# Hyena and mLSTM mixer: shifted rows issued from ScalarE's queue, and a new order of VectorE and ScalarE work

## The reference

```python
def hyena_mixer(u, conv_w, w1, b1, w2, b2, w3, freq, d_skip):
    u = short_conv3(u, conv_w).astype(jnp.float32)      # rows t-1, t, t+1 times three weights
    v, x1, x2 = jnp.split(u, 3, axis=-1)
    h = hyena_filters(L, w1, b1, w2, b2, w3, freq)      # each order divided by its sum of magnitudes
    d = d_skip.astype(jnp.float32)
    z = x1 * (long_conv(v, h[0]) + d[0] * v)            # long_conv: FFT, product, inverse FFT
    z = x2 * (long_conv(z, h[1]) + d[1] * z)
    return z

def even_mixer(xm, w_in, ...):
    u = xm @ w_in                                       # 1024 x 3600: Hyena v, x1, x2; q, k, v, o; gates
    y_hy = hyena_mixer(u[..., :3 * HY_W], ...)
    ...
    h, C, n, m = mlstm_bidir(heads(q), heads(k), heads(v), gates, C0, n0, m0)
    h = rmsnorm(h.transpose(0, 2, 1, 3), ml_norm_g).reshape(B, L, ML_W) * jax.nn.sigmoid(o)
    y = jnp.concatenate([y_hy, h], axis=-1) @ w_out
```

## Time and profile before

| | us |
|---|---|
| median of three runs | 1374.52 (1371.89 to 1374.98) |
| the profiled execution | 1374.98, its span 1373.1 |
| PE busy | 1321.2 (96%) |
| DVE busy | 1045.9 (76%) |
| ACT busy | 816.6 (59%) |
| POOL busy | 75.6 (6%) |
| DMA | 408.14 MB, mean 297 GB/s |

### The profile page before, as it was taken

The page is one execution under the profiler, slowest core; times in us unless marked ns, Lnnn a source line. Parts: engine busy times, 40 slices in busy tenths (PEclk is TensorE's granted clock), DMA queues, the critical chain, the costliest instruction groups (busy, mean ns, idle before and its releaser), DMA issues.

```text
span 1373.1 us, 16270 instructions
## 1 busy us (share of the span) xinstructions
PE 1321.2 (96%) x6307; PEld 1032.8 (75%) x6307; DVE 1045.9 (76%) x1011; ACT 816.6 (59%) x920; POOL 75.6 (6%) x81
## 2 busy tenths in 40 slices
PE   5999988999999989999999999999999999999997
PEld 2676646788886777788888888888888888888875
DVE  0584787555446753788998898998988988988996
ACT  2444324533335374677767767776777777777663
POOL 1102100000002000000000000000000000000370
PEclk9999999999999989999999999999999999999998
DMA  9979997855556633599999999999999999999992
GB/s 349 347 254 313 325 335 254 284 187 184 184 184 198 216 130 125 182 318 365 365 352 351 346 347 366 366 347 338 345 356 362 365 357 331 348 363 366 342 351 92
DMA packets 289591, 408.14 MB, mean 297 GB/s; under 512 B 15342, under 2 KB 223497, under 8 KB 289445
## 3 DMA queue, kind: packets, MB, share of 16 engines
q1 hardware_dynamic: 282048, 391.23, 83.8%
q0 software_dynamic: 3904, 11.59, 2.8%
q10 hardware_dynamic: 3556, 4.21, 0.9%
HBM read 401.99 MB, written 1.87 MB: 294 GB/s over the span
## 4 chain that ended last, share of the span: by engine, by line
PE 84%; DVE 8%; DMA 4%; ACT 1%; issue 1%; SPq 0%; POOL 0%; DVEq 0%; ACTq 0%
PE bank L1908 81%; DVE w_lo L550 3%; DMA raw<-in_w_ada 2%; PE bank L2258 2%; DMA Gb<-arena 1%; DMA raw<-in_ev_w_in 1%; PE bank L1966 1%; ACT w_hi L543 0%; DMA Gb<-gate_rows 0%; SPq L657 0%; ACT arena L1169 0%; DVE sml L1723 0%; PE bank L2379 0%; PE bank L2416 0%; DVE arena L1649 0%
## 5 line engine op out<-in xcount | busy, mean ns | idle before, releaser
L550 DVE TENSOR_TENSOR w_lo<-raw,w_hi 128x2048 fp32r<-128x2048 f32 (+1 forms) x238 | 549.0, 2309 | 157.0 <-ACT w_hi L543 155.4
L543 ACT CAST w_hi<-raw 128x2048 fp32r<-128x2048 f32 (+1 forms) x238 | 451.5, 1898 | 121.7 <-PE bank L1908 82.7
L1908 PE MATMUL bank<-w_hi,x_hi 128*128 128x512 f32 x1072 | 431.1, 402 | 7.5 <-DVE x_lo L1336 2.3
L1908 PE MATMUL bank<-w_lo,x_hi 128*128 128x512 f32 x1072 | 420.4, 392 | 0.0
L1908 PE MATMUL bank<-w_hi,x_lo 128*128 128x512 f32 x1072 | 419.3, 391 | 0.0
L1908 PEld LDWEIGHTS bank<-w_hi,x_hi 128*128 128x128 f32 x1072 | 201.3, 188 | 53.2 <-issue 8.7
L1908 PEld LDWEIGHTS bank<-w_hi,x_lo 128*128 128x128 f32 x1072 | 201.5, 188 | 45.2
L1908 PEld LDWEIGHTS bank<-w_lo,x_hi 128*128 128x128 f32 x1072 | 201.7, 188 | 38.8 <-issue 0.2
L550 DVE TENSOR_TENSOR w_lo<-arena,w_hi 128x2048 fp32r<-128x2048 f32 x88 | 203.0, 2307 | 33.1 <-ACT w_hi L543 32.9
L543 ACT CAST w_hi<-arena 128x2048 fp32r<-128x2048 f32 x88 | 168.3, 1912 | 28.8 <-PE bank L1908 28.8
L1908 PE MATMUL bank<-w_hi,g_hi 128*128 128x512 f32 x440 | 175.0, 398 | 3.4 <-DVE g_lo L1607 3.4
(11 more groups left out here) (300 smaller groups left out, 963.5 us busy)
## 6 DMA issues: line engine op xcount, KB each, us to landing
raw<-in_moe_w SPq DMA_DIRECT2D x352, 512.0 KB, 5.5
arena<-in_moe_w SPq DMA_DIRECT2D x176, 512.0 KB, 5.6
raw<-in_w_ada SPq DMA_DIRECT2D x96, 512.0 KB, 6.6
raw<-in_ff_w SPq DMA_DIRECT2D x66, 512.0 KB, 4.5
raw<-in_ev_w_in SPq DMA_DIRECT2D x28, 512.0 KB, 7.7
raw<-in_at_w_qkv SPq DMA_DIRECT2D x12, 512.0 KB, 5.1
raw<-in_ev_w_out SPq DMA_DIRECT2D x8, 512.0 KB, 5.7
Gb<-gate_rows POOLq DMA_DIRECT2D x8, 512.0 KB, 5.0
```

Of the source, the lines that this page charges most:

```text
L543: nc.scalar.copy(w_hi[:, t % SPL, c], place[:, c]).then_inc(hi_ok, 1)
L550: nc.vector.tensor_tensor(w_lo[:, t % SPL, c], raw_slot(n)[0][:, c], w_hi[:, t % SPL, c].bitcast(F32), ALU.subtract).then_inc(lo_ok, 1)
L1908: return pe.matmul(out, lhsT, rhs, start=start, stop=stop)
```

## The change

Four things change. The four shift DMAs of each block go from GpSimd's queue to ScalarE's own (`shift_rows(w)`), right behind the copies of that block's projection out of PSUM. On ScalarE the copy of projection 2 moves ahead of the magnitudes, the high part of IN[4] behind the logarithm of the gates, and the square root of the head squares ahead of `new_n` and `stage_rows(1)`. On VectorE both `normalised` move behind the low part of IN[6], `short_conv(2)` and `(3)` ahead of `weighted(2)` and `(3)`, `short_conv(4)` and `(5)` to both sides of `hyena_gate(0)`, and the head squares behind `fft_product(3)`. On TensorE two groups of idle products go from 13 and 5 to 7 and 9.

```diff
@@ GpSimd
-                pool.wait_ge(tj_t, 7 + 2 * w + 2)
-                pool.wait_ge(sh_z, 2)
-                uw = u[:, :, HW * w:HW * w + HW]
-                for r0, r1 in ((0, 112), (112, P - 1)):
-                    gp.dma_start(earlier[r0 + 1:r1 + 1], uw[r0:r1]).then_inc(sh_l, 16)
-                    gp.dma_start(later[r0:r1], uw[r0 + 1:r1 + 1]).then_inc(sh_l, 16)
@@ ScalarE
+            def shift_rows(w):
+                if w == 0:
+                    eng.wait_ge(sh_z, 2)
+                else:
+                    eng.wait_ge(cv_ok, 2 * w)
+                eng.wait_ge(tj_t, 7 + 2 * w + 2)
+                uw = u[:, :, HW * w:HW * w + HW]
+                for r0, r1 in ((0, 112), (112, P - 1)):
+                    eng.dma_start(earlier[r0 + 1:r1 + 1], uw[r0:r1]).then_inc(sh_l, 16)
+                    eng.dma_start(later[r0:r1], uw[r0 + 1:r1 + 1]).then_inc(sh_l, 16)
...
+            take_proj(2, two_heads(qT, 1))
             eng.wait_ge(f_tap, 1)
             for r in range(2):
                 sc.activation(mags[:, r, :], taps[:, 2 * r, :], ACT.Abs)
                 sc.activation(magb[:, r, :], taps[:, 2 * r + 1, :], ACT.Abs).then_inc(f_abs, 1)
-            take_proj(2, two_heads(qT, 1))
-            high(IN[4])
             eng.wait_ge(g_in, 1)
             link(sc.activation(rowq[:, 2, :], rowq[:, 1, :], ACT.Abs))
             link(sc.activation(rowq[:, 3, :], rowq[:, 2, :], ACT.Exp, scale=-1.0))
             sc.activation(rowq[:, 8, :], rowq[:, 3, :], ACT.Ln, bias=C("one", ROWS)).then_inc(g_f, 1)
+            high(IN[4])
             take_proj(3, two_heads(kT, 0))
...
             take_pair(7, block_of(u, 0))
+            shift_rows(0)
...
             take_pair(9, block_of(u, HW))
+            shift_rows(1)
...
             take_pair(11, block_of(u, 2 * HW))
+            shift_rows(2)
...
+            eng.wait_ge(hs_q, 1)
+            sc.activation(sml[:, 40:48], sml[:, 32:40], ACT.Sqrt, bias=C("eps"), scale=1.0 / HD).then_inc(hs_r, 1)
             eng.wait_ge(cs_ok, 3)
...
             stage_rows(1)
-            eng.wait_ge(hs_q, 1)
-            sc.activation(sml[:, 40:48], sml[:, 32:40], ACT.Sqrt, bias=C("eps"), scale=1.0 / HD).then_inc(hs_r, 1)
@@ VectorE
             low(IN[4])
-            eng.wait_ge(ld_h2, 16)
-            normalised(0)
             low(IN[5])
...
             low(IN[6])
+            eng.wait_ge(ld_h2, 16)
+            normalised(0)
+            low(IN[7])
             normalised(1)
-            low(IN[7])
...
             low(IN[12])
+            short_conv(2)
+            short_conv(3)
             weighted(2)
             weighted(3)
-            short_conv(2)
             low(IN[13])
-            short_conv(3)
...
             low(IN[14])
+            short_conv(4)
             hyena_gate(0)
+            short_conv(5)
...
             fft_product(1)
-            short_conv(4)
             hyena_gate(1)
             head_rows(0)
-            short_conv(5)
             head_rows(1)
...
             head_rows(3)
+            fft_product(3)
             link(v_.tensor_tensor(sq, hall, hall, ALU.mult))
             v_.tensor_reduce(sml[:, 32:40], ...).then_inc(hs_q, 1)
-            fft_product(3)
@@ TensorE
             ada_cols(0)
-            idle_products(1, 13)
+            idle_products(1, 7)
             ada_half(8)
-            idle_products(1, 5)
+            idle_products(1, 9)
             ada_half(9)
```

## The result

| | before | after |
|---|---|---|
| median | 1373.61 us (four runs) | 1390.65 us (four runs, 1389.34 to 1392.73) |
| ratio to before | 1 | 1.0127, 95% interval 1.0108 to 1.0144 |
| profiled execution, its span | 1374.98, 1373.1 | 1390.67, 1388.9 |

The change costs 17.4 us (14.8 to 19.8). The prediction said 1383.0, +8.5, with 1388.5 as its upper end: the sign was right, the size half. The page shows the same kernel: the chain has moved a point from VectorE to DMA and one to ScalarE.

What follows compares the result with a forecast made beforehand. It took TensorE to bound the kernel, with the stream and later VectorE deciding waits in the mixer. 4.7 + 1.7 + 0.7 + 0.3 + 1.7 - 0.6 = +8.5 us gave 1383.0 us; range 1377.5 to 1388.5.

Steps and rivals of the forecast that it cites:

- The magnitudes, +4.7: Product with IN[3] waits for its low part behind VectorE's additions, starting at 74.4 and not 69.66 us: +4.7 us.
- The clock, +1.7 in that hole: TensorE's granted clock falls to 0.50 in the new hole from 68.4 to 74.4 us: +1.7 us.
- Normalised +0.7: `normalised(0)` behind the low part of IN[6] makes TensorE wait for spectra 0, so IN[7] starts late: +0.7 us.
- idle products +0.3: Nine idle products instead of five end at about 40.0, after the tile's arrival at 39.74: +0.3 us.
- Rival 3: Fewer idle products lower the clock early, in the products of IN[0] and IN[1]: +2.5 us, 1385.5; chance 0.10.
- The shifts on ScalarE, cost nothing: Four issues per block put 1.8 us ahead of the high parts of IN[10], IN[12], IN[14], which wait anyway: nothing.
- The arrival of the rows, taken as 145: Block 1's rows reach VectorE at 145 (bounds 144 and 149), so `fft(0)` waits behind both convolutions: +1.7 us.
- Rival 2: The rows arrive no sooner, and `fft(0)` waits 5.9 us instead of 1.7: +4.2, 1387.2; chance 0.12.
- Convolutions 4 and 5 out of the way, the -1.3 within the -0.6: VectorE less loaded later gives back 0.2 and 1.1 of the 3.4 us of waits for the long convolution's products.
- The rest of that term: Late mixer: product 1.7 us sooner, squares 2.4 us ahead of the last gate; square root covered by VectorE's last operations.
- TensorE run without a gap there: From about 240 us TensorE has no gap, so whatever the mixer gains or loses reaches the end whole.

Runs made afterwards that it cites:

- part D: Kernel before with only both `normalised` behind the low parts of IN[6] and IN[7] and idle products 7 and 9 for 13 and 5: +0.4 us against before.
- e8: Changed kernel with idle products added in the four holes of TensorE that it opened: +12.8 us against the kernel before.
- e12: Kernel before with only the moves of both `normalised` and the new counts of idle products: +0.4 us against before.
- e2: Kernel before with only the twelve shift DMAs moved to ScalarE's queue: +5.1 us against before.
- C: Kernel before with only convolutions 2 and 3 ahead of `weighted(2)` and `(3)` on VectorE: +6.3 us against before.
- e6: Kernel before with only convolution 4 ahead of `hyena_gate(0)` and convolution 5 behind it: +12.5 us against before.
- e13: Kernel before with both edits of the short convolutions on VectorE and nothing else: +4.9 us against before.
- F: Kernel before with only the head squares behind `fft_product(3)` and the square root ahead of `new_n` and `stage_rows(1)`: +0.5 us against before.
- A: Kernel before with only ScalarE's copy of projection 2 ahead of the magnitudes and IN[4]'s high part behind the gates' logarithm: +5.8 us against before.
- B: Kernel before with only the shift DMAs issued from ScalarE's queue and not GpSimd's: +5.1 us against before.
- E: Kernel before with only convolutions 4 and 5 on both sides of `hyena_gate(0)`: +12.5 us against before.
- e5: Changed kernel with both edits of the short convolutions on VectorE undone: +7.4 us against the kernel before.
- e14: Changed kernel with each block's two large shift copies cut from 112 rows to 16, so rows arrive early (outputs wrong): +10.4 us against the kernel before.
- e15: Kernel before with idle products in most of TensorE's short waits: -1.9 us against before, median 1372.14 us.

## Why the prediction was half of it

**The magnitudes, +4.7: right.** In the trace after, the product with IN[3] is 4.9 us late and that with IN[6] 4.6, of which 0.4 were there ahead of IN[2]. Alone it is +5.8 (3.6 to 8.0), but with the wait of 3.12 us that part D removes.

**The clock, +1.7 in that hole: wrong place.** The clock did fall there (70.92 to 74.33), but what ran in it, the two sums (3.36 us instead of 1.9), was done when the low part of IN[3] was (74.5). It cost nothing. What cost were the low stretches behind waits that the prediction had too small or not at all: 1.6 us in `fft(0)`, 1.6 in `fft(1)`, 1.6 or more behind the turn of the rows. e8 sizes them together at 4.6, or 2.8 by the medians.

**Normalised +0.7, idle products +0.3: right** within what can be measured (e12: +0.4). Rival 3, the early low clock, came true in the changed kernel's trace (36.78 to 43.61): the product with IN[0] came 3.7 us late. Only 0.4 us of it was left at IN[2], since the stretch of 55.38 was gone in exchange, which is luck of that execution.

**The shifts on ScalarE, cost nothing: the first step that failed.** Alone they cost 5.1 (1.9 to 8.1). The step took 0.45 us per issue, about what one of SP's takes (median 0.47), where the trace has 0.6 to 1.7 on ScalarE, 3.3 to 4.1 per block. It reasoned that the split behind waited for its tile by 1.8 us anyway. Before, that of IN[10] did wait 1.80, but in e2 it was held 4.55 us. And it did not look at what stands behind the split: the spectra copies, GpSimd's state loads, and IN[12] beside them.

**The arrival of the rows, taken as 145: the second step that failed, and the dearest.** The prediction took the end of the range that the nearest row (12.5 us from issue to use) spoke against, on the ground that the 768 KB ahead were gone. They were not: GpSimd issued them at 141.63, 0.5 us ahead of the copies. The bound of 6.8 us below it was the landing of a copy of 60 KB; the shortest of a large one was 7.0. The rows took 13.4 us from the first issue (142.16 to 155.56). `fft(0)` waited 6.46 and not 1.7; with the low clock that is most of C's price. Rival 2, put at 0.12, gave 5.9 for this wait and should have been the forecast. The Trainium skill (DMA: Bandwidth & Descriptors, section Issuing engines are not separate DMA queues) says that DMAs from ScalarE, SyncE and GpSimd run on the same 16 DMA engines and interleave. The trace agrees in the main: the copies into `earlier` (three of 448 KB, three of 60 KB) landed 8.6 us after their issue from ScalarE (median of six), 9.3 from GpSimd, and the slower issues took the difference back. e6 and e13 show a larger difference, 11.6 or 7.4 us for the same copies from the same queue, with the stream's transfers issued ahead of them or behind.

**Convolutions 4 and 5 out of the way, the -1.3 within the -0.6: the third step that failed.** It counted VectorE's load and forgot the wait that moved with the convolution: `hyena_gate(0)` and `fft(1)` stood behind the rows of block 2. Alone this costs 12.5 us. In the changed kernel it shows as only 2.03 us, because C had made `fft(0)` late already. The rest of that term was a wash, as F measured: the square root was not covered, 2.73 us of staging against the 1.4 gained.

**What comes behind 240 us.** The prediction had TensorE run without a gap there. It waits there too (3.4 us in five waits for VectorE's L1607 alone, before and after alike), and the low stretches of the two profiled executions differ (two and four), which goes with the 2.6 us that came back.

**The sum.** A 5.8, B 5.1, C with E 4.9, D 0.4, F 0.5 make 16.7, against 17.4 measured. Each is uncertain by about 2 us and more, and A and B alone contain losses that the changed kernel has not or has smaller: A the wait that D removes, B the late landing of IN[12] (16.0 us from its issue in e2, 10.8 in the changed kernel). So the agreement is in part luck, and no proof that the parts don't act on each other. Shown in the changed kernel are the waits, their releasers and their sizes, and by e5 and e14 that the edits of the convolutions, through the late rows, carry 7 to 10 us of the loss. B's share inside the change stays open.

## What to carry to other kernels

When an instruction that waits for a transfer is moved ahead on its engine, list everything behind it and price the wait with the landing that the trace shows, not with the one that the change is meant to bring. A DMA issue is work of the issuing engine (here 0.6 to 1.7 us each on ScalarE): list what stands behind it, and which other engine's loads wait for that. Undoing one part of a change can make it slower still, so try pairs that meet at the same transfer before a part is called good or bad.

## What was not expected of the hardware

- The same two copies (448 and 60 KB) from the same queue landed in 11.6 us (median) with six of the stream's 512 KB transfers issued in the 4.3 us ahead of them, and in 7.4 us with the stream issued behind them.
- Four DMA issues in a row on ScalarE took 3.3 to 4.1 us in the changed kernel, the slowest 1.72 us, against 0.56 to 0.70 each on GpSimd in the kernel before.
- A low clock followed TensorE's waits of 1 to 13 us in the mixer in nearly every profile, for 3.4 to 13.7 us at a time, but not behind the same wait each time. With most of TensorE's short waits filled with idle products the profile of e15 had one such stretch before 600 us, that of before five.
